# A hybrid DeltaNet and attention block: ScalarE evicts before it converts, and steps of the next head's projection change places

## The reference

```python
h = rms_norm(x, norm_w);  z = h @ w_in          # 8 heads q,k,v,z_a; 16 attention heads; gates
# branch A, gated DeltaNet, 8 heads of 128, chunks of 64
qkv = silu(causal_depthwise_conv([qa, ka, va], conv_w))   # 4 taps
qa, ka = l2_normalize(qa), l2_normalize(ka)
beta = sigmoid(b_a);  g = -exp(a_log) * softplus(a_a + dt_bias)
oa = gated_delta_rule(qa, ka, va, g, beta)      # inverse of (I + N) by repeated squaring, state scan
ya = (rms_norm(oa, gdn_norm_w) * silu(za)) @ w_o_a
# branch B, sliding-window attention, 16 query heads on 2 key heads, window 128, sinks, T5 bias
yb = (softmax_with_sink(qb kb^T / 8 + bias) vb * silu(zb)) @ w_o_b
x = x + (sigmoid(gate_a) * ya + sigmoid(gate_b) * yb) @ w_out
out = rms_norm(x, final_norm_w)
```

## Time and profile before

| | us |
|---|---|
| median of 3 runs | 2969.01 (2966.41 to 2971.51) |
| the profiled execution | 2970.99 |
| its span, first to last instruction | 2969.2 |
| TensorE busy | 2815.3 (95%) |
| VectorE busy | 1423.1 (48%) |
| ScalarE busy | 959.4 (32%) |
| GpSimd busy | 392.6 (13%) |
| mean granted TensorE clock | 0.991 of full |

### The profile page before, as it was taken

How to read it: one execution, slowest core, us unless ns; L and a number is a source line. 1 busy time by engine, 2 the same in 40 slices (tenths; PEclk the granted TensorE clock), 3 DMA queues, 4 the chain that set the end, 5 groups by cost and what they waited for, 6 DMA issues and landing times.

```text
span 2969.2 us, 48770 instructions
## 1 busy us (share of the span) xinstructions
PE 2815.3 (95%) x19624; PEld 2290.2 (77%) x19624; DVE 1423.1 (48%) x3173; ACT 959.4 (32%) x2961; POOL 392.6 (13%) x237
## 2 busy tenths in 40 slices
PE   5988888899999999999999999999999999999997
PEld 4777767688887777778887777778888777777885
DVE  3666666523345666551316665662223556655122
ACT  3444444442223334331013343333111433343100
POOL 3323222234310010000000100000000000000000
PEclk9999999999999999999999999999999999999998
DMA  6444434378753332335654323334555232323463
GB/s 225 154 151 147 157 136 145 128 252 290 277 206 107 111 118 102 113 106 215 222 186 158 118 102 115 105 115 170 213 186 215 103 116 103 117 103 113 176 221 142
DMA packets 77552, 463.12 MB, mean 156 GB/s; under 512 B 13072, under 2 KB 17296, under 8 KB 29200
## 3 DMA queue, kind: packets, MB, share of 16 engines
q1 hardware_dynamic: 65520, 429.42, 40.6%
q10 hardware_dynamic: 11808, 30.57, 2.8%
HBM read 356.15 MB, written 103.81 MB: 155 GB/s over the span
## 4 chain that ended last, share of the span: by engine, by line
PE 81%; issue 9%; ACT 6%; DVE 4%; DMA 0%; POOL 0%; DVEq 0%; POOLq 0%; ACTq 0%; SPq 0%
PE bank L1104 20%; PE bank L1106 19%; PE bank L1105 19%; PE bank L1224 5%; PE bank L1213 3%; PE bank L1251 2%; PE bank L1198 2%; PE bank L1187 1%; PE bank L1304 1%; PE bank L1314 1%; PE bank L1258 1%; PE bank L1309 1%; ACT area L609 1%; ACT area L620 1%; PE bank L1319 1%
## 5 line engine op out<-in xcount | busy, mean ns | idle before, releaser
L1104 PE MATMUL bank<-hT_hi,w_sl 128*128 128x512 f32 x2144 | 911.1, 425 | 24.5 <-ACT qbd L559 23.2
L1106 PE MATMUL bank<-hT_hi,w_sl 128*128 128x512 f32 x2144 | 846.0, 395 | 0.0
L1105 PE MATMUL bank<-hT_lo,w_sl 128*128 128x512 f32 x2144 | 843.9, 394 | 0.0
L1104 PEld LDWEIGHTS bank<-hT_hi,w_sl 128*128 128x128 f32 x2144 | 406.8, 190 | 116.1 <-issue 46.8
L1106 PEld LDWEIGHTS bank<-hT_hi,w_sl 128*128 128x128 f32 x2144 | 405.6, 189 | 90.8
L1105 PEld LDWEIGHTS bank<-hT_lo,w_sl 128*128 128x128 f32 x2144 | 407.6, 190 | 57.9
L379 POOL TENSOR_TENSOR w_sl<-w_raw,w_sl 128x1024 fp32r<-128x1024 f32 x91 | 218.9, 2408 | 527.4 <-ACT w_sl L452 527.3
L757 DVE TENSOR_SCALAR area<-bank 128x256 f32<-128x256 f32 (+1 forms) x192 | 81.1, 422 | 296.9 <-PE bank L1224 181.0
L858 DVE SCALAR_TENSOR_TENSOR area<-zraw,stc,area 128x512 f32<-128x512 f32 x288 | 217.5, 755 | 3.3
L392 POOL TENSOR_TENSOR rqo<-qo,half 128x8 f32<-128x8 f32 x32 | 55.5, 1735 | 985.8 <-DVE qo L1008 985.8
L1224 PE MATMUL bank<-area 64*64 64x128 f32 (+1 forms) x3072 | 165.1, 247 | 0.0
(11 more groups left out here) (192 smaller groups left out, 4574.6 us busy)
## 6 DMA issues: line engine op xcount, KB each, us to landing
w_sl<-saved_w SPq DMA_DIRECT2D x273, 1024.0 KB, 4.8
saved_w<-w_sl SPq DMA_DIRECT2D x91, 1024.0 KB, 4.8
w_raw<-in_w_tiles SPq DMA_DIRECT2D x91, 512.0 KB, 5.8
area<-in_x ACTq DMA_DIRECT2D x8, 2048.0 KB, 9.9
out_y<-area ACTq DMA_DIRECT2D x4, 2048.0 KB, 7.3
bias_sb<-in_bias ACTq DMA_DIRECT2D x33, 128.0 KB, 2.7
fw<-in_final_w ACTq DMA_DIRECT2D x1, 512.0 KB, 10.6
stc<-in_step_const ACTq DMA_DIRECT2D x32, 6.5 KB, 2.2
```

What stands on the lines that cost most here:

```text
L1104: pe.matmul(dst, a_hi, b_hi, start=first, stop=False)
L1105: pe.matmul(dst, a_hi, b_lo, start=False, stop=False)
L1106: return pe.matmul(dst, a_lo, b_hi, start=False, stop=last)
```

## The change

ScalarE's `product` no longer converts; a new `refill(n)` converts tile n + 3 and stands behind the instruction that reads tile n's bank. The order of fills changes on ScalarE, VectorE and TensorE. VectorE makes the second logits before the corner and not behind r of chunk 0. L1023 signals a new semaphore, for which TensorE's transposes of v in the next head wait instead of the end of VectorE's head.

```diff
@@ scalar
             def product(n):
                 act.wait_ge(tile_done, n + 1)
-                if n + SLOTS < len(USES) and FRESH[n + SLOTS]:
-                    high_part(n + SLOTS)
+            def refill(n):
+                if rounds(n):
+                    high_part(n + SLOTS)
@@ prologue, after each tile's copy (for the third tile behind sp_in and L507's Ln)
+                refill(n)
@@ project
                     act.activation(zraw[:, i, CONV - 1:], bank[bk][:, :], ACT.Copy).then_inc(z_read[bk], 1)
+                    refill(n + i)
...
                 act.activation(qbd[DH:P, par, :, CH:P], zq[DH:P], ACT.Copy, scale=DH ** -0.5).then_inc(z_read[bk], 1)
+                refill(n + 3)
...
                     product(n + i + 1)
                     act.wait_ge(silu_ready[i - 2], n1)
                     act.activation(ez[i % 2], bank[bank_of(n + i + 1)][:, :], ACT.Tanh, scale=0.5).then_inc(tanh_z[i], 1)
+                    refill(n + i + 1)
@@ gates: refill(n) behind the tanh; ya, yb, out: refill(n) right behind product(n)
@@ head, scalar
                 probs_copy(0)
-                fill(1)
+                fill(2)
                 act.wait_ge(tz_done, n1)
                 act.activation(t11[0:CH], bch(7)[0:CH, :, 0:CH], ACT.Copy).then_inc(t11_ready, 1)
-                fill(1)
...
                 state(0)
                 softmax_exp(1)
+                fill(1)
                 state(1)
                 square_o(0)
                 fill(1)
                 state(2)
                 probs_copy(1)
+                fill(1)
                 square_o(1)
-                fill(1)
                 state(3)
@@ head, vector
                 quotient(0)
+                fill(1)
                 level(5)
-                fill(1)
                 diagonal()
                 gated(0)
+                fill(1)
                 dve.wait_ge(tz_done, n1)
                 copy(z_sb[0:CH], bch(5)[0:CH, :, 0:CH]).then_inc(z_ready, 1)
-                fill(1)
+                logits(1)
                 corner()
...
-                    if t == 0:
-                        logits(1)
-                    else:
+                    if t != 2:
                         fill(1)
...
-                    if t == 1:
+                    if t == 0:
+                        fill(2)
+                    elif t == 1:
                         quotient(1)
                         fill(1)
-                    elif t < NT - 1:
+                    elif t == 2:
                         fill(2)
...
                 dve.tensor_tensor(o_sb, o_sb, fo[:, :, None].to_broadcast([P, NT, P]), ALU.mult).then_inc(on_ready, 1)
-                fill(1)
+                fill(2)
                 dve.wait_ge(ot_done, n1)
...
-                ch.link(dve.scalar_tensor_tensor(zat, bank[4][:, :], gnw[:, 0:1], zat, ALU.mult, ALU.mult))
+                dve.scalar_tensor_tensor(zat, bank[4][:, :], gnw[:, 0:1], zat, ALU.mult, ALU.mult).then_inc(ot_read, 1)
+                dve.wait_ge(ot_read, n1)
@@ head, tensor
-                after(pe, head_dve_done, n1 - 1)
+                after(pe, ot_read, n1 - 1)
                 transposes(2, vv)
...
                 ins.then_inc(p_done, 1)
-                fill(2)
+                fill(4)
                 square(1)
```

More of the change, by code:

```diff
@@ L259, in build_program @@
         head_dve_done = sem("head_dve_done")
+        ot_read = sem("ot_read")
         sc_ready = sem("sc_ready")
@@ L330, in build_program @@
         act_pro = sem("act_pro")
-        DVE_PRO, DVE_HEAD, DVE_PROJ, ACT_PRO = 11, 21, 10, 3
+        DVE_PRO, DVE_HEAD, DVE_PROJ, ACT_PRO = 11, 20, 10, 3
         def after(eng, s, n):
@@ L499, in prologue @@
                 act.activation(kb[:, CH:CH + TB], bank[bank_of(n + 1)][:, :], ACT.Copy).then_inc(z_read[bank_of(n + 1)], 1)
+                refill(n + 1)
                 yield
@@ L507, in prologue @@
                 act.activation(pa[:, 1, :, :], pa[:, 4, :, :], ACT.Ln).then_inc(lns, 1)
+                refill(n + 2)
                 yield
```

## The result

| | before | after |
|---|---|---|
| median, us | 2970.26 (2966.41 to 2972.47, 4 runs) | 2855.30 (2855.14 to 2855.39, 4 runs) |
| profiled execution, us | 2970.99 | 2855.39 |
| mean granted clock | 0.991 | 0.997 |

The ratio is 0.9617, 95% interval 0.9603 to 0.9631. The forecast was 2872, with 97.6 us gained; measured were 115 (115.6 between the profiled executions). The sign and the main mechanism, fewer waits of TensorE and a fuller clock, were right. The gain was undersized by 17 to 18 us, and two parts of the argument, on evicting first and on the new semaphore, were wrong.

The account below looks back on a forecast made before the run. TensorE's queue plus its waits was taken as the bound. Blocks 1 to 3 42.9, block 0 46.9, clock 12.6, last heads -4.8: 97.6 us gained, 2873.4 profiled, about 2872 median; range 2856 to 2910, the forecast's own terms 2855 to 2888.

Parts of the forecast that it names:

- The bound and the split: TensorE's queue plus its waits set the end; five waits recurring per head, 60.2 us in block 0, 42.9 in blocks 1 to 3.
- 42.9 us of rows: Blocks 1 to 3: waits at L1213 (17.0), L559 (12.4) and L1304 (13.5) all go.
- the last heads: Each block's last head: y waits behind the fifth gate tanh, 0.93 us in three blocks, 2.0 in block 0; 4.8 lost.
- ScalarE's moves: Steps earlier in the head remove waits at L559 (12.4 and 10.8 us) and L1304 (13.5 and 4.5).
- The end of the head: Transposes of o: with two steps taken away TensorE still comes 1.8 us after the data, nothing paid in blocks 1 to 3.
- 46.9 + 12.6 - 2.0: Block 0: 60.2 - 7.7 - 5.6 = 46.9 us of waits, 12.6 of 18.6 clock regained, 2.0 lost in its last head.
- 0.7 was charged: Block 0, r of chunk 2: the quotient is still held by GpSimd's subtraction, 0.7 us in eight heads, 5.6 of 13.1 stay.
- The 1.1 charged at L1273: Block 0: 3.3 us of delay on VectorE's chain to L900 against 2.2 of room; 1.1 in seven heads, 7.7.
- Evicting first is free: Block 0: banks free 1.06 us sooner, conversions about 0.6 later, but converted tiles are wanted 11 us later, so no cost.
- the 0.27 at the first square: Block 0, L1213: of the 1.64 us wait, 0.27 remains after two more steps; left out as covered by a later term.
- The coin toss at L1018: Block 0: L1018 may lose the lock to GpSimd's subtraction, 1.3 us in seven heads; part of a rival at 2900, chance 0.17.
- The hand-over semaphore: Block 0: v's transposes wait only for L1023, not VectorE's head end, so L1187's 18.5 us goes in that form.

Follow-up runs that it names:

- three of the experiments: Changed kernel with, in turn, the two steps ahead of the first square undone (2890.12 us), converting first again (2880.55), VectorE's z_a SiLU ahead of the read of o (2871.40).
- the last tries to remove a wait: z_a SiLU ahead of o's read, on the changed kernel: 2871.40 us; conversion behind z_b tanh, 2864.63, and z_a SiLU between L1041 and L1042, 2859.94, on the 2851.4 kernel.
- the first experiment: Changed kernel with fill(2) ahead of the first square again, the fifth gate tanh of a block's last head taken behind chunk 3: 2890.12 us.
- one kernel: The 2851.4 us kernel (changed kernel, last heads' fifth gate tanh behind chunk 3) with VectorE's z_a SiLU between L1041 and L1042: 2859.94 us.
- the try before that: The 2851.4 us kernel (changed kernel, last heads' fifth gate tanh behind chunk 3) with the conversion behind the z_a tanh taken behind the z_b tanh: 2864.63 us.

## Why the prediction was right, and what it mis-sized

**The bound and the split** were right. The five waits per head were the thing to look at, and both parts, block 0 and blocks 1 to 3, gave what lay in them and more.

**Blocks 1 to 3, undersized by 14 us.** The sum had 42.9 us of rows less 2.8 for the last heads, 40.1; measured were 54.4. The term priced each wait by its row in the list. Three such waits have rows of 1.93 us and cost 2.59: 0.78 for the 0.70 at the first square, 1.75 for the 1.23 at the other two, and 0.06 that no experiment placed. The overlap of products before the wait and the slower first products behind it are booked as busy. Two rows of before, had I laid them beside a normal step, say it: after the earlier trace rows's spacing one expects 0.23 from one product to the next, and here it is 0.99 with an idle row of 0.59.

```profile
1157.03 0.40 PE L1106 MATMUL bank<-hT_hi,w_sl 128*128 128x512 f32 x1
1158.02 0.48 PE L1104 MATMUL bank<-hT_hi,w_sl 128*128 128x512 f32 x1 [0.59 <-ACT qbd L559]
```

**ScalarE's moves** were the main part: alone they gave 75 us. The waits for the q copy and at L1304 went, and no new wait at r or y came in blocks 1 to 3. VectorE's own new order and its moved logits were not timed alone.

**The end of the head** held: no wait at L1348 outside block 0's last head (0.6), so the two steps taken from there cost nothing.

**Block 0, undersized by 3 us, with errors in its parts.** The forecast's 46.9 + 12.6 - 2.0 = 57.5 stands against 60.5. The clock came back wholly (1.00 in the windows), 6 more than taken. The waits left are 10.7 + 3.0 + 5.1 = 18.8 against the 13.3 charged. At L1330 seven heads wait 0.49 each and the last 1.70, where 0.7 was charged. That the sum came within 3 us is partly luck, since these errors and the 25 us of the next paragraph are larger. The 1.1 charged at L1273 became 0.42 there, and 1.53 at the step behind the transposes of v. That was a misreading: I took both SiLU steps to go ahead of L1023, but VectorE has no fill behind r in chunk 2, so its count is one step behind and the z_a SiLU still comes behind the head's end.

**"Evicting first is free", wrong.** I gave it no gain of its own; it is worth 25 us, by the undoing and by itself. The banks were empty in time, as argued. In the changed kernel what it moves is when GpSimd subtracts, by 0.2 to 0.6 us, and so which VectorE operations are held: two of over 2 us in a head, and six without it. It also took the 0.27 at the first square that the forecast had left out: with converting first that row is 2.4 us in eight heads, with evicting first 0.3 in one.

**The coin toss at L1018** did not fall there: L1033 runs in 0.69 ahead of the subtractions, because ScalarE's tanh for the third SiLU waits for VectorE and its conversion comes later than I had it. It fell at L1041, by 20 ns, and well. The same operation lost in three of the experiments (2890, 2881 and 2871 us). The Trainium skill (SBUF — State Buffer, Who interferes with whom) says that the issue order decides who blocks; the 0.43 against 2.03 us of the same operation agrees.

**The hand-over semaphore, credited with L1187's 18.5 us, wrong.** It is worth nothing (2855.31). About half of L1187's wait went because VectorE's end comes sooner against TensorE (18.5 to 8.8 with the old semaphore); the rest was not saved but moved to the next step, with the z_a SiLU (10.7). The hold by GpSimd is behind both: without the subtraction neither kernel has such a wait.

**The last heads** cost 3.9 us, 4.8 were charged.

**The lower end of 2855** does not follow from the two terms that it names: 2872 less 6.0 for the clock and 7.7 for L1273 is 2858, so the stated range reached lower than its argument.

## What to carry to other kernels

Price a wait in a row of overlapping products by the distance between starts before and behind it, against the distance without a wait, and not by its idle row: here the rows held 1.93 of 2.59 us. Where two engines block each other, an edit that only shifts one of them by half a microsecond can be worth as much as the edit that it serves, so time each half alone. Before removing a wait, ask which end sets it, and whether the next wait hangs on the same end. And read the granted clock head by head: in the last tries to remove a wait, most of what was lost was clock and not waiting.

## What was not expected of the hardware

GpSimd's subtraction of 2.38 us holds even tiny VectorE operations: one of 128x4 elements took 2.38 us instead of 0.16. It goes the other way too: where VectorE's operation had started first, the two subtractions took 5.42 us together (the changed kernel), and 4.86 where they had (the first experiment). And the granted clock answers to waits of this size unevenly. At the same place in the program, a wait of 2.2 us was followed in some heads of one kernel by a granted clock of 0.97 and in others by 1.00, while each of the seven waits of 2.4 in the try before that was followed by 0.97. In the changed kernel, with waits of 1.53 and 0.4 us some 6 us apart, it stayed at 1.00. Why it falls in one and not in the next is left open.
